# A two-layer macaron block in split float32 on one core: bias load moved, its mask on VectorE, v halves first, another order in the first output unit, x first at the beginning

## What is computed

```python
def reference(x, ffn1_norm, ffn1_w_up, ffn1_w_down, mix_norm, w_in, na_rel_bias, w_branch_a,
              w_branch_b, w_out, ffn2_norm, ffn2_w_up, ffn2_w_down, final_norm):
    pos = jnp.arange(x.shape[1])
    for l in range(DEPTH):
        x = x + 0.5 * swiglu(rms_norm(x, ffn1_norm[l]), ffn1_w_up[l], ffn1_w_down[l])
        x = x + hybrid_mixer(rms_norm(x, mix_norm[l]), w_in[l], na_rel_bias[l],
                             w_branch_a[l], w_branch_b[l], w_out[l], pos)
        x = x + 0.5 * swiglu(rms_norm(x, ffn2_norm[l]), ffn2_w_up[l], ffn2_w_down[l])
    return rms_norm(x, final_norm)

def swiglu(x, w_up, w_down):
    gate, up = jnp.split(x @ w_up, 2, axis=-1)
    return (jax.nn.silu(gate) * up) @ w_down
```

## Time and profile before

| what | value |
| --- | --- |
| median of 3 runs | 1180.21 us (1179.6 to 1180.6) |
| the profiled execution's own time | 1182.51 us |
| its span, first to last instruction | 1180.7 us |
| TensorE busy | 1163.3 us (99%) |
| VectorE busy | 781.5 us (66%) |
| ScalarE busy | 588.7 us (50%) |
| GpSimd busy | 62.5 us (5%) |
| mean granted clock of TensorE | 0.996 |
| moved by DMA | 211.54 MB, mean 179 GB/s |

### The profile page before, as it was taken

How to read it: one execution, slowest core, us unless ns; L and a number is a source line. 1 busy time by engine, 2 the same in 40 slices (tenths; PEclk the granted TensorE clock), 3 DMA queues, 4 the chain that set the end, 5 groups by cost and what they waited for, 6 DMA issues and landing times.

```text
span 1180.7 us, 16070 instructions
## 1 busy us (share of the span) xinstructions
PE 1163.3 (99%) x6163; PEld 980.3 (83%) x6163; DVE 781.5 (66%) x992; ACT 588.7 (50%) x772; POOL 62.5 (5%) x84
## 2 busy tenths in 40 slices
PE   8999999999999999999999999999999999999997
PEld 6888887888888888888888888887888888888886
DVE  5766666755665776666676666677557567766665
ACT  6544444555544464444464444464555435544443
POOL 0011110110200000000000000001102000000000
PEclk9999999999999999999999999999999999999999
DMA  8666655653435465555556555655433445656551
GB/s 276 220 221 216 208 197 205 205 178 109 142 109 178 143 212 180 187 204 178 178 178 214 178 182 200 239 178 178 144 126 125 161 143 178 214 178 205 186 178 36
DMA packets 145601, 211.54 MB, mean 179 GB/s; under 512 B 7648, under 2 KB 112272, under 8 KB 145296
## 3 DMA queue, kind: packets, MB, share of 16 engines
q1 hardware_dynamic: 142960, 206.33, 51.5%
q0 software_dynamic: 1920, 3.20, 0.8%
q10 hardware_dynamic: 672, 1.37, 0.4%
HBM read 209.77 MB, written 4.19 MB: 181 GB/s over the span
## 4 chain that ended last, share of the span: by engine, by line
PE 91%; DVE 3%; DMA 2%; ACT 1%; issue 1%; SPq 0%; POOLq 0%; POOL 0%; DVEq 0%; ACTq 0%
PE banks L1139 23%; PE banks L1073 15%; PE banks L1075 15%; PE banks L1074 15%; PE banks L1137 13%; PE banks L1136 3%; PE banks L1285 2%; PE banks L1258 2%; PE banks L1270 1%; DVE gates L890 1%; DMA raw<-ffn_w_up_dram 1%; ACT w_hi L535 1%; PE banks L1248 1%; DMA raw<-w_in_dram 1%; PE banks L1111 1%
## 5 line engine op out<-in xcount | busy, mean ns | idle before, releaser
L760 DVE TENSOR_TENSOR w_lo<-raw,w_hi 128x2048 fp32r<-128x2048 f32 x190 | 434.9, 2290 | 188.9 <-ACT w_hi L535 188.9
L535 ACT ACTIVATE w_hi<-raw 128x2048 fp32r<-128x2048 f32 x190 | 363.5, 1915 | 240.8 <-PE banks L1075 236.8
L1139 PE MATMUL banks<-a_both,w_hi 128*128 128x512 f32 x1232 | 439.3, 396 | 0.0
L1137 PE MATMUL banks<-a_both,w_lo 128*128 128x256 f32 x1408 | 364.1, 279 | 0.0
L1137 PEld LDWEIGHTS banks<-a_both,w_lo 128*128 128x128 f32 x1408 | 265.4, 188 | 14.7
L1139 PEld LDWEIGHTS banks<-a_both,w_hi 128*128 128x128 f32 x1232 | 231.2, 188 | 47.3
L1073 PE MATMUL banks<-w_hi,a_both 128*128 128x512 f32 (+1 forms) x448 | 181.4, 405 | 0.4 <-DVE a_both L1035 0.4
L1075 PE MATMUL banks<-w_hi,a_both 128*128 128x512 f32 (+1 forms) x448 | 172.1, 384 | 0.0
L1074 PE MATMUL banks<-w_lo,a_both 128*128 128x512 f32 (+1 forms) x448 | 171.4, 383 | 0.0
L1073 PE MATMUL banks<-w_hi,hT_hi 128*128 128x512 f32 x320 | 124.9, 390 | 0.0
L1075 PE MATMUL banks<-w_hi,hT_lo 128*128 128x512 f32 x320 | 124.5, 389 | 0.0
(11 more groups left out here) (105 smaller groups left out, 1002.4 us busy)
## 6 DMA issues: line engine op xcount, KB each, us to landing
raw<-ffn_w_up_dram SPq DMA_DIRECT2D x172, 512.0 KB, 4.2
raw<-w_in_dram SPq DMA_DIRECT2D x92, 512.0 KB, 4.4
raw<-ffn_w_down_dram SPq DMA_DIRECT2D x88, 512.0 KB, 3.9
raw<-w_out_dram SPq DMA_DIRECT2D x16, 512.0 KB, 4.1
raw<-w_branch_b_dram SPq DMA_DIRECT2D x8, 512.0 KB, 4.1
bias_rows<-na_rel_bias_dram POOLq DMA_DIRECT2D x24, 128.0 KB, 4.4
bias<-bias_rows SPq DMA_DIRECT2D x2, 1536.0 KB, 7.5
raw<-ffn_w_up_dram SPq DMA_DIRECT2D x8, 256.0 KB, 5.3
```

Source lines behind the costliest of these rows:

```text
L535: act.activation(w_hi[slot][:, :], raw[slot][:, :], ACT.Copy).then_inc(hi_done, 1)
L760: dve.tensor_tensor(w_lo[slot][:, :], raw[slot][:, :], w_hi[slot][:, :].bitcast(F32), ALU.subtract).then_inc(lo_done, 1)
L1137: mm = pe.matmul(pair[:, b, 0:SEQ], w_lo[slot][:, at:at + P], a_hi[:, k, :], start=False, stop=False)
L1139: mm = pe.matmul(pair[:, b, :], w, both, start=False, stop=k == KT - 1)
```

## The change

Five edits, none of which changes a value that is computed (the mask's sums are the same ones).

1. **Bias load** (SP): the wait for `bias_spread` and the 1.5 MB load stand behind the six q/k units of the mixer, ahead of its unit 6.
2. **Mask**: GpSimd's eight additions and its waits for `consts_loaded` and `bias_loaded` are gone; VectorE makes two additions of 128x1536, in steps 7 and 8, behind `lo(9)` and `lo(10)`, the first after a wait for `bias_loaded`.
3. **v first** (all four feed-forward blocks, chunk 0): VectorE's order is u added, `lo(3)`, v added, wait for norm factors, u scaled, `lo(4)`, gate, product; ScalarE copies v's lower half right behind `hi(3)` and does `hi(4)` ahead of the tanh. The later chunks keep their order.
4. **First output unit**: TensorE takes the four groups as (0,0), (0,1), (1,0), (1,1) of (t, n); before it was (0,0), (1,0), (0,1), (1,1).
5. **x first**: identity and gain rows are issued by GpSimd, ahead of its memsets, so ScalarE's queue begins with x 1. ScalarE and VectorE split x 1 ahead of unit 0, whose first half is then split in two quarters with a semaphore for each; TensorE's first products wait quarter by quarter.

```diff
@@ SP
             for l in range(DEPTH):
                 feed_forward(0, l, F1_AT)
-
-                sp.wait_ge(bias_spread, 16 * DEPTH * 2 * BIAS_ROWS)
-                sp.dma_start(bias[:, :, :, :].rearrange("p h r k -> p (h r k)"),
-                             bias_rows.rearrange("l p h r k -> l p (h r k)")[l, :, :]).then_inc(bias_loaded, 16)
                 n0 = l * L_UNITS + M_AT
                 m = 0
                 for g in range(GROUPS):
                     for a in range(2):
                         unit(n0 + m, m % RING, qk_unit(l, g, a))
                         m += 1
+                sp.wait_ge(bias_spread, 16 * DEPTH * 2 * BIAS_ROWS)
+                sp.dma_start(bias[:, :, :, :].rearrange("p h r k -> p (h r k)"),
+                             bias_rows.rearrange("l p h r k -> l p (h r k)")[l, :, :]).then_inc(bias_loaded, 16)
@@ GpSimd
         def _(pool):
+            pool.dma_start(ident, consts[:, C_IDENT:C_ALL]).then_inc(ident_loaded, 16)
+            pool.dma_start(gain_rows[0:DEPTH * PHASES * KT, :],
+                           gains[0:LAST, :].rearrange("g (k p) -> (g k) p", p=P)).then_inc(gain_rows_loaded, 16)
...
-            pool.wait_ge(consts_loaded, 16)
             for l in range(DEPTH):
-                pool.wait_ge(bias_loaded, l * 16 + 16)
                 norm_factors(l * PHASES + 1)
-                for h in range(NA_HEADS):
-                    pool.wait_ge(split_free, RING + l * L_UNITS + M_AT + 4 + h)
-                    pool.tensor_tensor(bias[:, h, :, :], bias[:, h, :, :],
-                                       na_mask.unsqueeze(1).to_broadcast([P, BIAS_ROWS, GRID_W]),
-                                       ALU.add).then_inc(bias_ready, 1)
@@ ScalarE
-            act.dma_start(ident, consts[:, C_IDENT:C_ALL]).then_inc(ident_loaded, 16)
-            act.dma_start(gain_rows[0:DEPTH * PHASES * KT, :],
-                          gains[0:LAST, :].rearrange("g (k p) -> (g k) p", p=P)).then_inc(gain_rows_loaded, 16)
             load_x(act, 1)
...
                 u_lower(0)
                 hi(l, at, 3)
+                v_lower(0)
                 act.wait_ge(rows_turned, ff + 1)
                 act.activation(half_rstd_rows, bank[ROWS][:, 0:SEQ], ACT.Copy).then_inc(rows_ready, 1)
+                hi(l, at, 4)
                 tanh(0)
-                v_lower(0)
-                hi(l, at, 4)
...
             transposed_hi(0, 0)
-            first_hi(0, 0)
             transposed_hi(0, 1)
+            first_quarter_hi(0)
+            first_quarter_hi(1)
             first_hi(1, 0)
@@ VectorE
                 lo(l, at, 2)
-                u_half(0)
+                u_add(0)
+                lo(l, at, 3)
+                v_add(0)
+                dve.wait_ge(rows_ready, ff + 1)
+                u_scale(0)
+                lo(l, at, 4)
                 gate(0)
-                v_half(0)
-                lo(l, at, 4)
+                product(0)
...
                             if p == DIL_PAIRS and hh == 0:
-                                dve.wait_ge(bias_ready, (l + 1) * NA_HEADS)
+                                dve.wait_ge(bias_ready, (l + 1) * 2)
...
+                    if m in (VC_AT - 1, VC_AT):
+                        if m == VC_AT - 1:
+                            dve.wait_ge(bias_loaded, l * 16 + 16)
+                        h0 = (m - VC_AT + 1) * NA_HEADS // 2
+                        part = bias[:, h0:h0 + NA_HEADS // 2, :, :].rearrange("p h r k -> p (h r) k")
+                        dve.tensor_tensor(part, part, na_mask.unsqueeze(1).to_broadcast([P, NA_HEADS // 2 * BIAS_ROWS, GRID_W]),
+                                          ALU.add).then_inc(bias_ready, 1)
...
             transposed_lo(0, 0)
-            first_lo(0, 0)
             transposed_lo(0, 1)
+            first_quarter_lo(0)
+            first_quarter_lo(1)
             first_lo(1, 0)
@@ TensorE
-                    pe.wait_ge(part_lo, 1)
                     pe.wait_ge(xT_lo, 2)
-                    up(0, U_BANKS, FIRST)
+                    for b in range(2):
+                        for q in range(2):
+                            pe.wait_ge(part_lo, q + 1)
+                            up(0, U_BANKS, (2 * q, 2 * q + 1), blocks=(b,))
                     input_transposes(0, 3)
-                    pe.wait_ge(part_lo, 2)
+                    pe.wait_ge(part_lo, 3)
...
-                    for g, (t, n) in enumerate(GROUP4):
+                    for g in (0, 2, 1, 3) if j == 0 else range(4):
+                        t, n = GROUP4[g]
                         if j == 0 and n == 0:
                             pe.wait_ge(mT_lo, l * 4 + t + 1)
```

More of the change, by code:

```diff
@@ L207, in build @@
         hi_done = sem("hi_done")
+        first_arrived = sem("first_arrived")
         part_arrived = [sem(f"part_arrived{h}") for h in range(4)]
@@ L1038, in merged_lo, with first_quarter_lo @@
                                   ALU.subtract).then_inc(mT_lo, 1)
+            def first_quarter_lo(q):
+                dve.wait_ge(part_hi, q + 1)
+                part = slice(q * NB, (q + 1) * NB)
+                dve.tensor_tensor(w_lo[0][:, part], raw[0][:, part], w_hi[0][:, part].bitcast(F32),
+                                  ALU.subtract).then_inc(part_lo, 1)
             def first_lo(a, h):
@@ L1124, in input_products, with up @@
                         part(a, t, (2, 3))
-            def up(slot, pair, ks, between=None):
-                for b in range(2):
+            def up(slot, pair, ks, between=None, blocks=(0, 1)):
+                for b in blocks:
                     if b == 1 and between is not None:
```

46 lines of the change are left out of this document (25 added, 21 removed).

## The result

The changed kernel takes 1174.39 us (median of 5, 1173.3 to 1174.85) against 1180.21 (1179.6 to 1180.76): ratio 0.995, 95% interval 0.9938 to 0.9962, so 4.5 to 7.3 us less. (The ratio is taken over all executions, not from the two medians, so gains by ratio and by medians can differ by a microsecond.) The forecast was 1170.9 with 1169.3 to 1174.3: faster, as said, but by 5.8 us instead of 9.3, and just outside the range. Two later comparisons of the same kernel gave 0.9946 (1175.30, interval 0.9932 to 0.996) and 0.9939 (1174.39, 0.9925 to 0.9953).

What follows compares the result with a forecast made beforehand. TensorE is busy 99% of the span, so only its stops and lower-clock time can be won. 2.2 + 1.7 + 3.2 + 1.1 + 0.4 + 0.7 = 9.3 us off 1180.2 gives 1170.9, range 1169.3 to 1174.3.

Steps and rivals of the forecast that it cites:

- The stop at 190: Layer 0's mixer: TensorE's wait for unit 0's weight, delayed by the bias load, goes; 2.2 us.
- Rope: Second rope: GpSimd's mask additions lengthen a VectorE product; without them TensorE's four stops go, 4 x 0.81 = 3.2 us.
- rival A: The rope stop stays, through another reader than GpSimd or another wait there: 1174.1 us, chance 0.10.
- rival D: The stop before the mixer's unit 0 stays, because something else than the bias load keeps it: 1174.8 us, chance 0.05.
- rival E: Slower: the moved bias load stops the v units, with lower clock following; 1182.3 us if 4 us late; chance 0.03.
- 1.7 us: Layer 0's mixer: the half-speed clock right behind the wait for unit 0 goes with that stop; 1.7 us.
- differences of it are taken off the median: Gains summed on the profiled execution (1182.5 us), 2.3 above the median, are subtracted from the median, 1180.2.
- rival C: The lower clock stays or comes elsewhere: 1.7 us back, 1172.6 us, chance 0.06.
- 1.1 us gone: First feed-forward block, chunk 1: v first removes TensorE's gap between u and v products; 1.1 us.
- 0.4 for x first: Beginning: x 1 issued 0.9 us earlier lets TensorE start sooner; 0.4 us taken, bounds 0 and 1.0.
- Rival B: Late beginning: identity or gains from GpSimd's queue land after about 7.2 us; 1174.0, or 1172.3 without clock loss; chance 0.10.
- I cost the move at 0: Bias load now ahead of the mixer's v units: unit 6 still lands 1.7 us early, so no cost in either layer.

Runs made afterwards that it cites:

- experiment 4: Kernel before with the mask moved to VectorE, GpSimd's additions and waits gone, bias load left in place: 1177.07 us, ratio 0.9966 to the kernel before.
- experiment 1: Kernel before, unchanged, run again with the clock of each execution: 1180.84 us, ratio 1.0.
- experiment 7: Kernel before with only v first (chunk 0 of the four feed-forward blocks): 1179.59 us, ratio 0.9992 to the kernel before.
- experiment 8: Kernel before with only x first, identity and gains on GpSimd's queue: 1183.69 us, ratio 1.0017 to the kernel before.
- experiment 6: Kernel before with only the other group order in the first output unit: 1180.06 us, ratio 0.9994 to the kernel before.
- experiment 3: Kernel before with the bias load moved and GpSimd's norm factors put ahead of its wait for that load, mask still on GpSimd: 1178.82 us, ratio 0.9973.
- experiment 9: Changed kernel without x first: 1174.33 us, ratio 0.9941 to the kernel before; again 1173.73 us, ratio 0.9941.
- experiment 10: Changed kernel without v first and x first: 1174.70 us, ratio 0.9947 to the kernel before.
- experiment 2: Kernel before with only the bias load moved behind the q/k units, mask and its wait still on GpSimd: 1195.63 us, ratio 1.012.
- experiment 5: Kernel before with the bias load moved and the mask on VectorE, without the other three edits: 1175.92 us, ratio 0.9948 to the kernel before.
- experiment 12: Changed kernel with identity and gains on ScalarE's queue and ScalarE's first squares ahead: 1174.06 us, ratio 0.9934 to the kernel before; again 1174.17 us, ratio 0.9944.
- experiment 11: Changed kernel with identity and gains back on ScalarE's queue: 1174.40 us, ratio 0.9944 to the kernel before; again 1174.18 us, ratio 0.9938.

## Why the prediction was wrong in size

**What held.** The stop at 190: 2.2 forecast, 2.28 in the traces. Rope: 3.2, and 3.3 in W to the last, or 3.2 by experiment 4. The long product is one of two in each of the second and third ropes that lie beside a GpSimd addition; the one before it, 230.52 to 231.21 and nearly whole inside the addition, takes 0.69. It is the addition that is longer there, 1.51 us against 1.01 with no product beside it:
```profile
225.15 1.01 POOL L495 TENSOR_TENSOR bias<-bias,cst 128x384 f32<-128x384 f32 x1 [14.39 <-PE banks L1075]
```
So first GpSimd lost half a microsecond, then VectorE 0.83. That each waits for the other in turn fits the page "SBUF — State Buffer" of the Trainium skill ("Who interferes with whom"). Output unit: 0.7, measured 0.9 to 1.0 in the traces. The mask's cost of 0 and its 1.76 us held. Rivals A, D and E did not come. (The low bounds 1.9 for the stop and 0.6 for the output unit have no working in the prediction.)

**First failed step: "1.7 us" for the lower clock, and "differences of it are taken off the median".** The first half was right for the profiled execution: V to W shrank by 3.94, which is 2.28 + 1.66. But it isn't in the median. All traces of kernels that keep the stop:

| kernel | start to start at the stop | V to W | the execution, above its kernel's median |
|---|---|---|---|
| before | 2.47 | 168.19 | 2.3 |
| experiment 1 | 2.73 | 168.47 | 2.7 |
| experiment 7 | 2.89 | 168.58 | 4.5 |
| experiment 8 | 2.90 | 168.66 | 2.0 |
| experiment 6 | 2.67 | 166.81 | 0.0 |
| experiment 4 | 0.95 | 165.07 | -1.0 |
| 14 traces without the stop | 0.3 | 164.20 to 164.38 | -0.9 to 1.1 |

The four executions with the lower clock are those that lie 2 us and more above their medians; the one with the whole stop and no lower clock lies on its median. Each of the four is also longer than all other executions measured with it, so they are no fair sample. The stop itself varies too, from 0.95 to 2.90.

The mean clock of every execution is on record, traced or not, and says more. Beside the experiments the kernel before ran 95 times. In 43 of these the mean clock is 0.998 or more, which no trace with the lower clock behind the stop has (0.995 to 0.997), and none of the 43 lies over 1.5 us above the median of its comparison; of the other 52, 17 do. The 18 with 0.996 or less lie 1.3 above, as their middle value. So the lower clock behind the stop comes in some executions only: in at most 52 of 95, and in about 18 if a mean of 0.996 or less means it. A half clock at the beginning lowers the mean too, so 0.997 can't be told apart. The 43 lie 0.3 us below the medians, as their middle value: by this estimate the median holds some 0.3 of the lower clock, and not 1.7. So I subtracted from the median a loss that it has only in small part. The offset of 2.3 us was in the table from the start; I took it for something that before and after share, and after's is 0. Experiment 3's interval (2.1 to 4.3) can't decide it: it holds the stop without the lower clock and with it. The prediction gave rival C ("the lower clock stays or comes elsewhere") 0.06, and the low bound 1.4.

**Second failed step: "1.1 us gone" for v first, and 0.4 for x first**, together 1.5, in the traces -0.2, and in the times nothing that can be told (experiments 9 and 10). My sum gave v first the same value as low and as high bound, from the rows of one execution. The traces show two limits on V. Without the edit, V follows the start of ScalarE's split of unit 3 by 7.05 us. ScalarE's rows in experiments 2 (the `w_hi` split in the old order) and 5:
```profile
22.59 1.92 ACT L534 ACTIVATE w_hi<-raw 128x2048 fp32r<-128x2048 f32 x1 [0.81 <-DMA raw<-ffn_w_up_dram]
```
```profile
23.41 1.92 ACT L526 ACTIVATE w_hi<-raw 128x2048 fp32r<-128x2048 f32 x1 [1.91 <-DMA raw<-ffn_w_up_dram]
```
V is at 29.64 and 30.46; before it is 23.08 and 30.13, and in experiment 8 25.73 and 32.79. In all nine traces of the old order the distance is 7.05 or 7.06. With the edit the chain is 2.07 shorter, by the one trace where it binds, experiment 12's second:
```profile
24.80 1.91 ACT L527 ACTIVATE w_hi<-raw 128x2048 fp32r<-128x2048 f32 x1 [3.88 <-DMA raw<-ffn_w_up_dram]
```
and V is 29.79, 4.99 later, with TensorE waiting 0.9 us for the addition for v even so. But then TensorE's own work binds: V comes 17.6 us (up to 17.75) behind the first product in eight of the ten traces with the edit and the fillers. What the edit wins is the difference of the two limits: in before 30.13 - (11.56 + 17.62) = 0.95, in experiment 3, where the weights landed sooner, 29.41 - (11.71 + 17.62) = 0.08 (estimates from these rows). And both starting points move from execution to execution, with the same code ahead of them: the first product from 11.54 to 13.45, the split of unit 3 from 22.36 to 23.98. For the split it is the landing of the weights (the DMA share reads 1.05 to 1.10 up to 13 us). The first product goes with the clock: in the eight traces whose fillers all stand 0.22 us apart it comes at 11.25 to 12.25, in the eleven where four or more of the ten stand 0.43 apart at 11.69 to 14.04. The changed kernel's execution with 14.04 shows how. VectorE has its first two quarters ready at about 13.1 and 13.69,
```profile
12.41 1.28 DVE L1057 TENSOR_TENSOR w_lo<-raw,w_hi 128x512 fp32r<-128x512 f32 x2
```
but TensorE is in its second five fillers, the first of them at half speed, until 14.04. A gain of 0.1 to 1.0 us in a start that scatters by 1.6 to 1.9 is below what these runs can tell.

**Rival B came in part.** I had said "the gains come in by 6.5 at the latest". They were issued at 2.1, behind the identity, not near 0.8, and landed 5.3 us later, longer than any of the earlier trace rows. (The fixed 2.0 us plus bytes of the Trainium skill's page "DMA: Bandwidth & Descriptors" would have had them in by about 4.3, an estimate; the trace disagrees by three.) By its own rows the cover was 1.3 us, not 1.5: 10.57 less the 3.5 of ScalarE's work is 7.1. TensorE waited 2.70 us for the gains, and the first product came 1.1 later than before; but with the gains back at 4.73 it still came at 12.43 in experiment 11, where the clock was at half as well, so how much of the 1.1 is the gains' is open. Alone the edit costs 2.0 us in the time (experiment 8); in its trace the v chain, with unit 3 split at 25.73, gives nothing back. With v first the kernel is within 0.2 to 1.1 us of those with the gains on ScalarE's queue (experiments 11 and 12). That v first pays for x first would explain why neither shows in the whole, but experiment 7 shows no gain of v first to pay with; it is argued, not shown.

**A step right by luck: "I cost the move at 0".** I listed the queues that the load was moved past (the v units) and never asked who waits for `bias_loaded` itself. Experiments 2 and 3 price that omission at 17 us (1195.63 against 1178.82); the mask's edit happened to remove the waiter.

**The count by medians:** of the forecast 9.3, the stop 2.2, the rope 3.2 and the output unit 0.7 to 1.0 stay, 6.1 to 6.4, and the beginning gives about 0. Measured in three comparisons: 5.8, 5.3 and 7.3 by the medians, 5.9, 6.4 and 7.2 by the ratio. The 0.3 of lower clock estimated above fits in between; the scatter of the comparisons is too large to tell more.

## What to carry to other kernels

Where the profiled execution lies some microseconds above the median, look in its rows for a loss of that size before any difference is taken off the median: a stretch of lower clock is the first suspect. A second profile of the same kernel need not tell it (here it had the same stretch); the clock and time of all executions did. A stop ends at the later of two chains; what an edit on one of them wins is the distance to the other, and near the beginning, where both hang on DMA landings, its low bound is 0. When a transfer is moved, list those who wait for its semaphore as well as the queues that it passes, and what is queued behind them: here that was worth 17 us. At a start, read the clock from the spacing of equal matmuls.

## What the runs showed that I had not expected

- Waiting of one length, at one place, in one code: behind it 0.53 and 0.59 of the clock for 3.5 us, or 1.00.
- The beginning has several courses with the same code. In the changed kernel the view of stretches gives the clock as 0.51 from 9.0 to 12.4 us in one execution and as 1.00 in another, whose first product came later (14.04 against 12.68). The 1.00 is not to be trusted there: the fillers stand 0.43 us apart (five in 2.34 us, experiment 11), as at half speed, against 0.22 at full. The slower start had the slower clock for longer.
- One small DMA of the gains: 2.9 us from ScalarE's queue, 5.3 to 6.0 from GpSimd's, issued 0.9 us later behind the same x and weights.
